# Three pairs of gating-value chunks by seven products of a two by two division

## The reference

```python
proj = xn @ w_in
uv = jax.nn.gelu(proj[..., :2 * GMLP_WIDTH])
zg = proj[..., 2 * GMLP_WIDTH:]
u, v = jnp.split(uv, 2, axis=-1)
v = rms_norm(v, v_g)
...
mixed = jnp.einsum('gts,bnsgc->bntgc', ws, vc) + jnp.transpose(b_s)[None, None, :, :, None]
y = u * mixed * jax.nn.silu(zg)
```

## Time and profile before

| | us |
|---|---|
| runs, median of 3 (lowest, highest) | 2567.65 (2567.27, 2569.45) |
| the profiled execution, its time | 2567.76 |
| its span, first to last instruction | 2565.9 |
| TensorE busy | 2559.5 |
| VectorE busy | 1675.4 |
| ScalarE busy | 1273.7 |

### The profile page before, as it was taken

One profiled execution on the slowest core, in us unless ns is written; L12 is line 12 of the kernel. 1 busy time (PEld: TensorE's weight loads), 2 busy tenths in 40 slices (PEclk: granted clock), 3 DMA queues, 4 the chain that ended last, 5 costly groups with the idle time before them and its releaser, 6 DMA issues.

```text
span 2565.9 us, 29320 instructions
## 1 busy us (share of the span) xinstructions
PE 2559.5 (100%) x11461; PEld 2121.6 (83%) x11461; DVE 1675.4 (65%) x1949; ACT 1273.7 (50%) x1527; POOL 34.9 (1%) x56
## 2 busy tenths in 40 slices
PE   9999999999999999999999999999999999999999
PEld 7888888888888888888888888888888888888887
DVE  5646564566666666676876876555577668578576
ACT  6554443444545555455444444444465455455453
POOL 1000000000000000000000000000020000000000
PEclk9999999999999999999999999999999999999999
DMA  8767776676777777777565787666667667667673
GB/s 272 215 188 209 207 205 192 198 207 198 216 214 201 215 196 203 222 221 225 164 193 168 217 222 209 200 200 199 225 188 220 208 194 216 204 201 233 196 224 137
DMA packets 534793, 527.41 MB, mean 206 GB/s; under 512 B 294896, under 2 KB 297824, under 8 KB 534656
## 3 DMA queue, kind: packets, MB, share of 16 engines
q1 hardware_dynamic: 531856, 518.09, 67.9%
q0 software_dynamic: 2384, 6.93, 1.1%
q10 hardware_dynamic: 416, 0.52, 0.1%
HBM read 488.24 MB, written 2.10 MB: 191 GB/s over the span
## 4 chain that ended last, share of the span: by engine, by line
PE 99%; DMA 0%; DVE 0%; ACT 0%; issue 0%; SPq 0%
PE bank L2119 31%; PE bank L2120 31%; PE bank L2121 31%; PE bank L2183 1%; PE bank L2182 1%; PE bank L2184 1%; PE bank L2301 1%; PE bank L2290 1%; PE bank L2280 1%; DMA t_stage<-in_a_w_in_dram 0%; PE bank L2223 0%; PE bank L2229 0%; PE bank L2236 0%; PE bank L2361 0%; PE bank L2348 0%; PE bank L2374 0%
## 5 line engine op out<-in xcount | busy, mean ns | idle before, releaser
L1164 DVE TENSOR_TENSOR t_wl<-t_stage,t_wh 128x1024 fp32r<-128x1024 f32 x850 | 1030.8, 1222 | 688.4 <-ACT t_wh L656 685.2
L656 ACT ACTIVATE t_wh<-t_stage 128x1024 fp32r<-128x1024 f32 x851 | 892.7, 1057 | 861.7 <-PE bank L2121 827.2
L2119 PE MATMUL bank<-t_wl,t_xth 128*128 128x512 f32 x2480 | 972.2, 392 | 0.4 <-DVE t_xtl L1206 0.4
L2121 PE MATMUL bank<-t_wh,t_xtl 128*128 128x512 f32 x2480 | 965.3, 389 | 0.0
L2120 PE MATMUL bank<-t_wh,t_xth 128*128 128x512 f32 x2480 | 965.1, 389 | 0.0
L2121 PEld LDWEIGHTS bank<-t_wh,t_xtl 128*128 128x128 f32 x2480 | 465.5, 188 | 97.3
L2119 PEld LDWEIGHTS bank<-t_wl,t_xth 128*128 128x128 f32 x2480 | 465.6, 188 | 97.1 <-DVE t_xtl L1206 0.9
L2120 PEld LDWEIGHTS bank<-t_wh,t_xth 128*128 128x128 f32 x2480 | 465.6, 188 | 95.7 <-issue 0.2
L2119 PE MATMUL bank<-t_wl,t_yth 128*128 128x512 f32 x914 | 355.6, 389 | 0.0
L2120 PE MATMUL bank<-t_wh,t_yth 128*128 128x512 f32 x914 | 355.1, 389 | 0.0
L2121 PE MATMUL bank<-t_wh,t_ytl 128*128 128x512 f32 x914 | 355.1, 389 | 0.0
(11 more groups left out here) (340 smaller groups left out, 1236.4 us busy)
## 6 DMA issues: line engine op xcount, KB each, us to landing
t_stage<-in_a_w_in_dram SPq DMA_DIRECT2D x192, 512.0 KB, 4.3
t_stage<-in_w_in_dram SPq DMA_DIRECT2D x178, 512.0 KB, 4.2
t_stage<-in_b_w_in_dram SPq DMA_DIRECT2D x128, 512.0 KB, 4.4
t_stage<-in_w_down_dram SPq DMA_DIRECT2D x91, 512.0 KB, 4.8
t_stage<-in_w_up_dram SPq DMA_DIRECT2D x88, 512.0 KB, 4.4
t_stage<-in_a_w_out_dram SPq DMA_DIRECT2D x64, 512.0 KB, 4.2
t_ubuf<-in_w_up_dram SPq DMA_DIRECT2D x40, 512.0 KB, 4.5
t_ubuf<-in_w_down_dram SPq DMA_DIRECT2D x37, 512.0 KB, 5.2
```

Source lines behind the costliest of these rows:

```text
L656: e.activation(wh[:, j % N_SPLIT], stage[s], ACT.Copy).then_inc(*hi(j))
L1164: e.tensor_tensor(low, src, high.bitcast(F32), ALU.subtract).then_inc(*lo(j))
L2119: e.matmul(o, h, w_l, start=start, stop=False)
L2121: return e.matmul(o, l, w_h, start=False, stop=stop)
```

## The change

The pairs (v2, v3), (v4, v5) and (v6, v7) are put ahead of the seven of the down projection. The order of the places becomes:

- 0 to 7 chunk 0; 8 to 11 chunk 1, then P1 at 12, P5 at 14, P6 at 16, P7 at 18, and between them (13, 15, 17, 19) the last four groups of chunk 1;
- 20 chunk 2, 21 P2, 22 chunk 3, 23 P3, 24 chunk 2, 25 P4, 26 chunk 3, then 27 and 29 chunk 2, 28 and 30 chunk 3, and 32, 34 chunk 2, 36, 38 chunk 3 with the next pair's P1, P5, P6, P7 at 31, 33, 35, 37;
- 39 to 57 the same for chunks 4 and 5, 58 to 72 for chunks 6 and 7 with nothing placed ahead at the end; `z` begins at 73 in place of 64.

The old slot numbers are mapped by `when` to the place that comes at the same share of TensorE's work: 13 to 16, 14 to 17, 20 to 25, 22 to 28, 27 to 33, 31 to 39, 34 to 42, 37 to 46, 40 to 49, and from 64 on by nine more.

Two staging buffers are added from chunk 1 to the begin of chunk 6, in space that is free then. The sums of the tokens are made from the high and low parts (`split_sums`, then `sum_high` on ScalarE and `sum_low` on VectorE). A chunk in a pair is no longer taken out by the GELU: VectorE adds banks and joined quarter into the value buffer (`v_sum`), then the GELU runs there in place.

```diff
 def halved_pairs():
-    return [(("down", q, c), ("down", q, c + 1)) for q in range(4) for c in (0, 2) if (q, c) != (3, 2)]
+    return ([(("v", c), ("v", c + 1)) for c in (2, 4, 6)] +
+            [(("down", q, c), ("down", q, c + 1)) for q in range(4) for c in (0, 2) if (q, c) != (3, 2)])
...
+    opens = {("up", 0, 0): [(N_STAGE + i, N_STAGE, lambda: prod.at("soft_weigh", 1, 2)) for i in range(N_MORE)]}
+    closes = {}
+    if ("v", 2) in first_of:
+        opens["v", 1] = [(7, N_STAGE, None), (8, N_STAGE, None)]
+        closes["v", 6] = (7, 8)
...
# ScalarE
+        def sum_high(*key):
+            m = next(m for m in range(len(pairs)) if sums_of(m)[0] == key)
+            _, high, low, raw = sums_of(m)
+            e.wait_ge(*vec.at("sums", *key))
+            e.activation(high.rearrange("p k s -> p (k s)"), raw, ACT.Copy).then_inc(*xhi("sums", *key))
+        def apart(m, after=None):
+            slot(where[m, P1] + 1)
+            e.wait_ge(*used.at(where[m, P1]))
+            if after is not None:
+                e.wait_ge(*after)
+            e.activation(quarters(m)[0], banks[4], ACT.Copy).then_inc(*act("first", m))
...
             for i in range(2):
-                e.activation(v_tile(c, i), accs("v", c)[i], ACT.Gelu_apprx_tanh,
-                             scale=sA[:, i:i + 1]).then_inc(*act("v", c, i))
+                if ("v", c) in pair_of:
+                    e.wait_ge(*vec.at("sum", "v", c, i))
+                e.activation(v_tile(c, i), v_tile(c, i) if ("v", c) in pair_of else accs("v", c)[i],
+                             ACT.Gelu_apprx_tanh, scale=sA[:, i:i + 1]).then_inc(*act("v", c, i))
...
                 squares(hres[:, i, cols(c)], ssq[:, i, c:c + 1], "x", c, i)
-        slot(14)
+            if c == 1:
+                sum_high("v")
+        apart(first_of["v", 2])
+        slot(when(14))
         v_evac(0)
         for c in range(1, 8):
             slot(end("v", c))
...
             v_evac(c)
+            if c in (2, 4):
+                apart(first_of["v", c + 2], vec.at("sum", "v", c, 0))
...
# VectorE
-        slot(13)
+        slot(10)
+        split_sums(xth, xtl, mo[:, 0, 0:1024], mo[:, 0, 1024:2048], "v")
+        slot(12)
+        sum_low("v")
+        slot(when(13))
         e.wait_ge(*square.at("x", 3, 1))
         norm_scale(sA, hA, ssq, 4, D, "sA")
...
+        def v_sum(c):
+            slot(end("v", c))
+            e.wait_ge(*used.at(end("v", c) - 1))
+            for i in range(2):
+                e.tensor_tensor(v_tile(c, i), accs("v", c)[i], quarters(pair_of["v", c])[2 * (c % 2) + i],
+                                ALU.add).then_inc(*vec("sum", "v", c, i))
+        slot(end("v", 1))
+        together(first_of["v", 2])
+        slot(when(20))
...
         e.tensor_tensor(gmix, gc[:, 32:48], gc[:, 48:64], ALU.mult).then_inc(*vec("gmix"))
+        v_sum(2)
         for p, n in ((0, 31), (1, 34)):
-            slot(n)
+            slot(when(n))
             e.wait_ge(*(prod.at("clear") if p else ws_in.at("ws")))
             for q in (2 * p, 2 * p + 1):
                 e.transpose(buf[2 + p][:, q % 2].rearrange("p (b g s) -> p b g s", b=4, g=4),
...
+            if p == 0:
+                v_sum(3)
+                together(first_of["v", 4], vec.at("sum", "v", 3, 1))
...
-        slot(64)
+        for c in (4, 6):
+            v_sum(c)
+            v_sum(c + 1)
+            if c == 4:
+                together(first_of["v", 6], vec.at("sum", "v", 5, 1))
+        slot(when(64))
...
# what frees a chunk's banks
+        if kind == "v" and name in pair_of:
+            return vec.at("sum", *name, 1)
...
# TensorE
-        products(27)
+        products(when(27))
         t = bank_of(5)
```

More of the change, by code:

```diff
@@ L265, in _program, with when @@
     first = {chunk[0]: where[chunk[0], 4 if chunk[0] in pair_of else 0] for chunk in chunks}
-    loads_, source = [], {}
+    up0 = first["up", 0, 0]
+    same_time, at_ = [], 0
+    for u, (m, own) in enumerate(units):
+        ahead = [] if u + 1 == len(units) or units[u + 1][0] is None else [1] * 4
+        mixed = [x for n, g in enumerate(own) for x in ahead[n - len(own) + 4:n - len(own) + 5] * (
+            n >= len(own) - 4) + [2 if g[0] in place else 1]]
+        plain_ = 16 if m is not None else len(own)
+        begins = [sum(mixed[:n]) for n in range(len(mixed) + 1)]
+        for n in range(plain_):
+            t = n * sum(mixed) / plain_
+            same_time.append(at_ + next(x for x, b in enumerate(begins) if b >= t))
+        at_ += len(mixed)
+    assert at_ == N
+    def when(n):
+        return same_time[n]
+    loads_, source, last_of = [], {}, {}
+    opens = {("up", 0, 0): [(N_STAGE + i, N_STAGE, lambda: prod.at("soft_weigh", 1, 2)) for i in range(N_MORE)]}
[3 more added lines that the diff above has]
+        closes["v", 6] = (7, 8)
     idle = [(-N_STAGE + i, i, None) for i in range(N_STAGE)]
@@ L291, in _program @@
     for j, (name, k) in enumerate(home):
-        if (name, k) == (("up", 0, 0), 0):
-            for i in range(N_MORE):
-                idle.append((j - N_STAGE, N_STAGE + i, ("soft_weigh", 1, 2)))
+        if name in opens and j == first[name]:
+            idle += [(j - lead, s, after) for s, lead, after in opens[name]]
+        if name in closes and j == first[name]:
+            last_of.update({s: after for _, s, after in idle if s in closes[name]})
+            idle[:] = [x for x in idle if x[1] not in closes[name]]
         if name in place:
-            source[j] = load_of(chunks[place[name]], plain_rows(k, 1024 // chunks[place[name]][5]), j, ("lo", j))
+            source[j] = load_of(chunks[place[name]], plain_rows(k, 1024 // chunks[place[name]][5]), j, lambda j=j: lo.at(j))
             continue
@@ L1090, in up_high @@
                 slot(end("up", q, c) + 5)
[L1091 to L1100, removed]
+                sum_high("up", q)
         e.wait_ge(*vec.at("sF"))
@@ L1271, in short_norm, with sums, split_sums, sum_low @@
                                    op1=ALU.mult).then_inc(*vec(*name))
+        def sums(x, raw, *key):
+            t = x.rearrange("p (n e) (i s) -> p e i n s", e=2, i=2)
+            a11, a21, a12, a22 = t[:, 0, 0], t[:, 0, 1], t[:, 1, 0], t[:, 1, 1]
+            s1, s2, s3, s4 = (raw[:, 256 * f:256 * f + 256].rearrange("p (n s) -> p n s", n=2) for f in range(4))
+            e.tensor_tensor(s1, a21, a22, ALU.add).then_inc(*vec())
+            e.tensor_tensor(s3, a11, a21, ALU.subtract).then_inc(*vec())
+            after_own()
+            e.tensor_tensor(s2, s1, a11, ALU.subtract).then_inc(*vec())
+            after_own()
+            e.tensor_tensor(s4, a12, s2, ALU.subtract).then_inc(*vec("sums", *key))
+            after_own()
+        def split_sums(xh, xl, x, raw, *key):
+            e.tensor_tensor(x, xh[:, 0:4, :].rearrange("p k s -> p (k s)").bitcast(F32),
+                            xl[:, 0:4, :].rearrange("p k s -> p (k s)").bitcast(F32), ALU.add).then_inc(*vec())
+            after_own()
+            sums(x.rearrange("p (k s) -> p k s", k=4), raw, *key)
+        def sum_low(*key):
+            m = next(m for m in range(len(pairs)) if sums_of(m)[0] == key)
+            _, high, low, raw = sums_of(m)
+            e.wait_ge(*xhi.at("sums", *key))
+            e.tensor_tensor(low, raw.rearrange("p (k s) -> p k s", k=4), high.bitcast(F32),
+                            ALU.subtract).then_inc(*xlo("sums", *key))
+        def together(m, after=None):
+            one, three_, two, four_ = quarters(m)
+            slot(where[m, P6] + 1)
+            e.wait_ge(*used.at(where[m, P6]))
+            e.wait_ge(*act.at("first", m))
+            if after is not None:
+                e.wait_ge(*after)
+            e.tensor_tensor(two, banks[6], one, ALU.add).then_inc(*vec("u2", m))
+            slot(where[m, P7] + 1)
+            e.wait_ge(*used.at(where[m, P7]))
+            e.wait_ge(*vec.at("u2", m))
+            e.tensor_tensor(three_, banks[7], two, ALU.add).then_inc(*vec("u3", m))
+            e.tensor_tensor(two, banks[5], two, ALU.add).then_inc(*vec("v", "pair", m))
+            e.wait_ge(*vec.at("u3", m))
+            e.tensor_tensor(four_, banks[5], three_, ALU.add).then_inc(*vec("w", "pair", m))
         e.memset(blank, 0.0).then_inc(*vec("blank"))
@@ L2433, in tensor @@
         name = ("w_out", 3)
[L2434 to L2435 removed]
+        products(up0 - 4)
+        for j in range(up0 - 4, up0):
             e.wait_ge(*lo.at(j))
```

296 lines of the change are left out of this document (143 added, 153 removed).

## The result

The changed kernel takes 2571.59 us (median of 22 runs, 2570.37 to 2572.95), the kernel before on the same chip 2567.61 (22 runs, 2567.10 to 2569.68): 1.0013 times as long, 95% interval 1.0007 to 1.0019. It is 4.0 us slower; the interval leaves out 1, so the loss is real, though small: it lies within the 0.2% named in the prediction and 3.6 us above the forecast of 2568.0. The profiled execution took 2571.58, with a span of 2569.8 (before 2565.9).

What follows compares the result with a forecast made beforehand. TensorE, 99% of the span, was taken to bound the kernel. Savings of 4.08 and 0.3 us against 4.75 us of new waits gave net +0.4, so 2568.0 us; range 2563.2 to 2573.0.

Steps and rivals of the forecast that it cites:

- Saved: On TensorE: 18 matmuls fewer, 4.08 us, and the wait for the first GELU gone, 0.3 us.
- P5, place 14: First pair: P5 late by 0.3 us behind the sums of the tokens and their splitting; bounds 0 and 1.5.
- Chunk 2, place 20: Chunk 2 due at 59.4 us, second GELU half done at 57.6: on time, no wait.
- rival B: Transfers before 56 us land late and hold up conversions and the GELU: 2574.5 us; chance 0.10.
- Place 24: Remainder 24 on VectorE, behind four joins, ends at 67.85 us, due 67.5: late by 0.35 us.
- Place 33: Second pair's P5 waits for VectorE's copies of the parameter transposes out of bank 5: 0.85 us; bounds 0.5 and 2.
- Place 41: Chunk 5 waits for VectorE's additions for chunk 3 behind two spatial-weight transposes: 2.75 us, the largest; bounds 0 and 4.
- Place 43: Chunk 3's GELU waits for the additions, so conversion and remainder 43 come late: 0.3 us.
- Third pair and place 62: Same chain without sine and transposes: 0 for the third pair, bounds 0 and 0.5; place 62 late by 0.2 us.
- rival D: TensorE's clock falls to 1.2 GHz after a wait, costing 1.4 to 4 us: 2569.4 to 2572; chance 0.05.
- Rival A: Queues looser than walked, all places on time, saving without new waits: 2563.3 us; chance 0.18.
- Rival C: ScalarE's detour ahead of conversion 39 dearer by two extra pauses of 1.4 us: 2570.8 us; chance 0.05.

Runs made afterwards that it cites:

- the scrap GELU: Changed kernel plus one GELU on 64 scrap columns ahead of ScalarE's wait for the norm's scale, so the table loads early: 2570.32 us.
- the run with the wait of 2.0: Changed kernel with sine and cosine and their table load moved on ScalarE from chunk 2 to ahead of chunk 7's GELU: 2569.41 us.
- the doubled transposes: Changed kernel with VectorE's two transposes of spatial weights ahead of chunk 3's additions made twice, same data: 2573.99 us.

## Why the prediction was right or wrong

The forecast said no change that can be told, by a saving of 4.4 us that waits of 4.75 eat up, and in kind that is what the kernel does: 4.0 us slower, still within 0.2%, with the waits at the places named. But the losses are 8.0 us and not 4.75. That the verdict held has some luck in it: 1.1 us more, less than the slow stretch differs between two profiled executions, would have passed the 0.2%. The distance of 3.6 us has four parts: a wait with no term (place 22), a term that was too small (place 41), the clock, and the restarts.

- **Saved**: right, 18 matmuls and the first GELU's wait (0.26 against 0.3).
- **P5, place 14**: 0.30, as predicted. The walk holds in its steps, too: conversion 14 ended at 42.0 (42.2), the remainder of the sums at 46.9 (47.05).
- **Chunk 2, place 20**: on time, as predicted; its load was issued at 45.78 and landed at 50.0, so rival B, late transfers, did not happen. But I stopped there. **Place 22**, chunk 3, waits for the next GELUs; I had named it only within rival B and had no term for it. I let the first GELU follow the scale at once. In the earlier trace rows the function table of the sine is loaded with nothing waited for, and I gave the one ahead of the first GELU no term. It is queued behind the wait for the scale: 1.28 us more, a wait of 0.81 at place 22. This is the step that failed, and the scrap GELU gave it back. The trace of before had the load to read, right ahead of the first GELU and behind the late conversion of the earlier trace rows:

```profile
50.38 1.28 ACT L719 ACT_TABLE_LOAD   x1
51.67 0.69 ACT L719 ACTIVATE t_vreg<-bank,t_scl 128x512 f32<-128x512 f32 x1
```

- **Place 24**: wait 0.37 (0.35). **Place 33**: 0.75 (0.85), and taking the transposes away returned 0.8.
- **Place 41**: the mechanism right in each link but one, 0.5 too small. Chunk 5 waited for the addition behind the two transposes (2.03, has 2.06). Counted from the start of place 34 at 93.36, the first transpose began at 15.0 (predicted 14.5), TensorE was due at 14.96 (15.0). The wait was 3.28. The missing part is between the two table loads:

```profile
94.70 1.28 ACT L800 ACT_TABLE_LOAD   x1
95.99 0.31 ACT L800 ACTIVATE t_sinb<-t_pool 128x128 f32<-128x128 f32 x1
96.21 0.29 ACT L801 ACTIVATE t_cosb<-t_pool 128x128 f32<-128x128 f32 x1
97.05 1.28 ACT L778 ACT_TABLE_LOAD   x1 [0.55 <-DVE t_vreg L1412]
```

  The second one stands behind the wait for VectorE's addition, which this change put in front of the GELU: 0.55, again a table load that doesn't run ahead of a wait. The same error as at place 22.
- **Place 43**: its 0.3 is covered in the changed kernel by the slow matmuls ahead of it; where they are absent it is there (0.33).
- **Third pair and place 62**: 0.08 (0) and 0.33 (0.2).
- **The clock, rival D**, to which I gave one chance in twenty: it happened, on top of my sum and not in place of it. Behind the wait of 3.28 us the clock was at 1.2 GHz for most of 3.8 us, 1.4 us lost; I had priced it at 1.4 to 4. No wait of that length was in the trace of before, so its chance could not be read there, but as a consequence of my own longest term it deserved far more. The Trainium skill (TensorE: Matmul & The Clock Gate, "What's actually happening") speaks of an idle TensorE being throttled; this trace agrees, with 0.55 in the row of 112 us.
- **Restarts**: about 0.1 after each of seven waits, 0.7 in all, which I counted only for the wait that went.
- **Rival A**, no new waits: false for this order of the queues; with other orders the waits between 40 and 200 us came down to 1.6 us, 1.8 us short of its number (2565.07 against 2563.3).
- **Rival C**, a drain for each switch of table: no. The sine begins 0.01 after its table load ends (95.99 here; in the trace of before 75.55, behind the load of 74.26 in the earlier trace rows). The Trainium skill (ScalarE: Activation LUTs, "What ACT_TABLE_LOAD costs") adds a drain of about 1380 ns; the trace does not show it, and the trace decides.

Summed: 0.81 for place 22, 0.52 at place 41, 1.4 for the clock, 0.7 for restarts, less 0.3 at place 43, is 3.1 of the 3.6; the rest is small differences at the other places and distances too short to list.

## What to carry to other kernels

Where an engine has no gap, fewer instructions for it pay only if every queue that feeds it stays ahead: walk each queue place by place to the next use of what it delivers, and one place beyond the one that seems safe. A wait taken away uncovers the next in another queue (place 41, then 43, then 60, then 42), so the gain of a fix is to be read from the ledger of all gaps and not from the one that it closes. And a long wait can cost twice, by itself and by the clock behind it: here the one of 3.28 us did. A function table that has to be loaded belongs in the walk as a step of its own, at the place where its activation stands and behind whatever that activation waits for.

## What the runs showed of the hardware

- In the profiled executions the matmuls after TensorE's waits of 0.8, 1.36, 1.5, 1.85 and 2.0 us came at the full 2.4 GHz (the times of the run with the wait of 2.0 leave open whether they always did). After 3.28 us came matmuls at 1.2 GHz: 7 distances of 0.43 in two profiles, with the first two or three still short, and 12 in a third, slow from the first on; there the clock is 0.87 over the wait itself (107.2 to 110.6) and 0.50 over 110.6 to 116.4. After 5.36 us it was 13, from the first on, in an execution 1.3 us above its median. The window of the doubled transposes, columns as above:

```profile
114.00:120.50 6.50, 6.37 (x15) 5.01 (x16) 5.75 (x8) 5.98 (x10) 0.00 (x0) 0.51 0.54 90
```

- A table load is queued behind the semaphore wait of the activation that needs it (55.37 after 2.85 us idle; 97.05 after 0.55). An activation of the same function on a few columns ahead of the wait hides 1.28 us of it.
- The first matmul after a wait is followed at 0.30 to 0.34 in place of 0.23 while the clock is full, and at 0.6 (0.60 and 0.59) where it had fallen.
- Eight sends of 64 KB held SyncE's queue for 5.5 to 8.1 us, with 512 KB loads queued behind them. In the changed kernel one such send has a median of 0.64 us in the queue and at most 1.58, a single load 0.37.
